# The three looped recurrent units of a one-core hybrid decoder kernel, written out

## What is computed

```python
def step(state, inp):                       # per chunk of 64 tokens and head
    qc, kc, vc, gc = inp
    b = jnp.cumsum(gc, axis=2)
    o_inter = jnp.einsum('bhck,bhkv->bhcv', qc * jnp.exp(b), state)
    ...
    scores = jnp.einsum('bhtk,bhtsk,bhsk->bhts', qc, decay, kc)
    o_intra = jnp.einsum('bhts,bhsv->bhtv', scores, vc)
    k_dec = kc * jnp.exp(b_last - b)
    new_state = jnp.exp(b_last[:, :, 0, :])[..., None] * state + \
        jnp.einsum('bhsk,bhsv->bhkv', k_dec, vc)
    return new_state, o_inter + o_intra
...
o_hg = o_hg * lax.rsqrt(jnp.mean(o_hg * o_hg, axis=-1, keepdims=True) + NORM_EPS) * g
o_hg = o_hg.reshape(B, S, HG_WIDTH) * jax.nn.silu(hg_z)
```

## Time and profile before

| | |
|---|---|
| time, median of 3 runs | 1389.83 us (1387.75 to 1391.33) |
| the profiled execution's own time | 1390.81 us |
| its span in the trace | 1389.0 us |
| TensorE busy | 1311.9 us (94%) |
| VectorE, ScalarE, GpSimd busy | 725.4, 465.1, 433.7 us |
| mean granted TensorE clock | 0.987 of full speed |

### The profile page before, as it was taken

How to read it: one execution, slowest core, us unless ns; L and a number is a source line. 1 busy time by engine, 2 the same in 40 slices (tenths; PEclk the granted TensorE clock), 3 DMA queues, 4 the chain that set the end, 5 groups by cost and what they waited for, 6 DMA issues and landing times.

```text
span 1389.0 us, 24238 instructions
## 1 busy us (share of the span) xinstructions
PE 1311.9 (94%) x8520; PEld 1144.1 (82%) x8520; DVE 725.4 (52%) x1885; ACT 465.1 (33%) x1328; POOL 433.7 (31%) x441
## 2 busy tenths in 40 slices
PE   5999989999999999889999999999999988999997
PEld 5989988998999799888878877887888776778886
DVE  5837674684687367510455454545555455243332
ACT  5621221122212111111454544444544446321111
POOL 5732343233324212120143333333433343112000
PEclk9999999999999999999999999999999999999999
DMA  6520122023002201332354445544544566535431
GB/s 212 149 80 20 47 81 76 20 83 102 23 31 84 84 20 50 97 104 80 73 145 132 114 105 140 132 114 105 155 132 105 145 161 170 168 110 163 143 127 61
DMA packets 121713, 143.92 MB, mean 104 GB/s; under 512 B 20352, under 2 KB 86400, under 8 KB 121600
## 3 DMA queue, kind: packets, MB, share of 16 engines
q1 hardware_dynamic: 119200, 138.46, 35.0%
q10 hardware_dynamic: 2400, 3.93, 1.1%
HBM read 87.56 MB, written 29.62 MB: 84 GB/s over the span
## 4 chain that ended last, share of the span: by engine, by line
PE 41%; DMA 6%; DVE 3%; issue 2%; POOL 2%; SPq 2%; ACT 1%; ACTq 0%; POOLq 0%; DVEq 0%
PE bank L760 4%; PE bank L788 4%; PE bank L762 4%; PE bank L761 4%; PE bank L790 4%; PE bank L789 4%; PE bank L919 3%; PE bank L866 3%; PE bank L859 2%; PE bank L911 2%; PE bank L880 1%; DMA qd<-turned 1%; DMA ks<-turned 1%; PE bank L888 1%; DMA tab<-in_rope 1%
## 5 line engine op out<-in xcount | busy, mean ns | idle before, releaser
L627 PE MATMUL bank<-w_hi,u_hi 128*128 128x256 f32 x768 | 222.7, 290 | 8.6 <-POOL w_lo L1180 4.5
L628 PE MATMUL bank<-w_lo,u_hi 128*128 128x256 f32 x768 | 219.3, 286 | 0.0
L629 PE MATMUL bank<-w_hi,u_lo 128*128 128x256 f32 x768 | 219.2, 285 | 0.0
L1361 DVE TENSOR_TENSOR room<-room 128x256 f32<-128x256 f32 (+6 forms) x386 | 137.1, 403 | 41.3 <-POOL room L1244 37.6
L627 PEld LDWEIGHTS bank<-w_hi,u_hi 128*128 128x128 f32 x768 | 149.4, 195 | 11.2 <-POOL w_lo L1180 4.5
L628 PEld LDWEIGHTS bank<-w_lo,u_hi 128*128 128x128 f32 x768 | 149.5, 195 | 0.2
L629 PEld LDWEIGHTS bank<-w_hi,u_lo 128*128 128x128 f32 x768 | 149.3, 194 | 0.0
L760 PE MATMUL bank<-u_hi,w_hi 128*128 128x512 f32 x256 | 109.6, 428 | 5.5 <-issue 4.0
L627 PE MATMUL bank<-u_hi,w_hi 128*128 128x512 f32 x256 | 101.2, 395 | 7.3 <-issue 3.7
L1361 DVE TENSOR_TENSOR t<-bank,tab 128x512 f32<-128x512 f32 x64 | 42.5, 685 | 120.2 <-DMA tab<-in_rope 58.7
L788 PE MATMUL bank<-u_hi,mT_hi 128*128 128x512 f32 x256 | 102.1, 399 | 2.7 <-DVE mT_lo L1361 2.7
(11 more groups left out here) (169 smaller groups left out, 2950.6 us busy)
## 6 DMA issues: line engine op xcount, KB each, us to landing
qd<-turned SPq DMA_DIRECT2D x64, 256.0 KB, 4.8
stage<-in_w_groups SPq DMA_DIRECT2D x44, 256.0 KB, 3.8
room<-in_x SPq DMA_DIRECT2D x16, 512.0 KB, 4.3
values_gates<-vg_tile SPq DMA_DIRECT2D x64, 128.0 KB, 1.7
room<-values_gates SPq DMA_DIRECT2D x16, 512.0 KB, 4.5
tab<-in_rope SPq DMA_DIRECT2D x16, 512.0 KB, 6.2
wide<-mix_weights SPq DMA_DIRECT2D x32, 256.0 KB, 3.9
xr<-in_x SPq DMA_DIRECT2D x16, 512.0 KB, 5.0
```

Of the source, the lines that this page charges most:

```text
L627: nc.tensor.matmul(dst, lhs_hi(k), rhs_hi(k), start=(k == 0), stop=False)
L628: nc.tensor.matmul(dst, lhs_hi(k), rhs_lo(k), start=False, stop=False)
L629: last = nc.tensor.matmul(dst, lhs_lo(k), rhs_hi(k), start=False, stop=(k == KT_N - 1))
L1361: return nc.vector.tensor_tensor(dst, a_, b_, op)
```

## The change

On each engine the loop over the first three units becomes an ordinary Python loop over all four, so that the same function is written out four times, with `u` a number each time. Nothing else is touched: the steps, their order, buffers and semaphores are those of before, and each unit waits for the same values. SP's helper `after` counts a semaphore up behind a wait on a register's value, and with numbers it does so no more.

```diff
--- before.py
+++ after.py
@@ -434,9 +434,8 @@
                         phase1_store(u + 1, i, last)
 
 
-            with sp.Fori(0, HG_UNITS - 1) as u:
-                hg_unit(u, False)
-            hg_unit(HG_UNITS - 1, True)
+            for u in range(HG_UNITS):
+                hg_unit(u, u == HG_UNITS - 1)
 
             def load_mixed(t):
                 sp.dma_start(mx[t % MX_SLOTS][:, :], mixed_dram[t * P:(t + 1) * P, :]).then_inc(mx_landed[t % MX_SLOTS], 16)
@@ -724,9 +723,8 @@
                     elif kind == "T":
                         phase1_tile(u + 1, b, "hgrn")
 
-            with pe.Fori(0, HG_UNITS - 1) as u:
+            for u in range(HG_UNITS):
                 hg_unit(u)
-            hg_unit(HG_UNITS - 1)
 
 
             def filler_matmuls(kind, n, part):
@@ -1041,9 +1039,8 @@
                     elif kind == "T":
                         phase1_tile(u + 1, b, "hgrn")
 
-            with act.Fori(0, HG_UNITS - 1) as u:
+            for u in range(HG_UNITS):
                 hg_unit(u)
-            hg_unit(HG_UNITS - 1)
 
 
             def queries_keys_hi(n):
@@ -1255,9 +1252,8 @@
                     elif kind == "T":
                         phase1_tile(u + 1, b, "hgrn")
 
-            with pool.Fori(0, HG_UNITS - 1) as u:
+            for u in range(HG_UNITS):
                 hg_unit(u)
-            hg_unit(HG_UNITS - 1)
 
 
             for i in range(4):
@@ -1541,9 +1537,8 @@
                         last.then_inc((out_done0, out_done1)[b % 2], 1)
                 restart()
 
-            with dve.Fori(0, HG_UNITS - 1) as u:
+            for u in range(HG_UNITS):
                 hg_unit(u)
-            hg_unit(HG_UNITS - 1)
 
 
             def classes(ap):
```

## The result

| | before | after |
|---|---|---|
| time, median (range, runs), taken side by side | 1391.38 us (1384.2 to 1398.3, 12) | 1381.24 us (1377.0 to 1383.7, 12) |
| ratio, 95% interval | | 0.9931 (0.9911 to 0.9952) |
| the profiled execution's own time, its span | 1390.81, 1389.0 us | 1379.92, 1377.9 us |
| its mean granted clock | 0.987 | 0.992 |

What follows compares the result with a forecast made beforehand. TensorE, busy 1311.9 of 1389.0 us, was taken as the bound; 1.1 us gained at two seams, nothing elsewhere, took the profiled 1390.8 to 1389.7 us, the median to 1388.7 us, range 1385.8 to 1391.5 us (8 in 10).

Steps and rivals of the forecast that it cites:

- The seams of the changed kernel: Between units: P0 follows O3 without a jump, new waits appear before P1, whose f group starts at 20.02 us.
- the data's chain: From O3 through squares, root, Z3, its store, weight loads and splits to the sigmoids that free P1's f group's bank.
- the mark: Start of O3's first matmul at the end of a unit, from which the prediction counts times at each seam.
- a gain of 1.1 us: At the first two seams together, P1's f group starts earlier: 40.04 us in sum against 41.13 us.
- 21.09, 20.04: Starts in us of P1's f group after O3's first matmul, first and second seam, one profile of the kernel before.
- my rival on the clock: At the seams, longer waits behind P0 and P1 would lower TensorE's clock: slower, 1394.1 us; chance 0.05.
- L688 and the register instructions: Waits before the last block's transposes stay 1.3 to 1.5 us; dropping address arithmetic on VectorE, ScalarE and GpSimd gains nothing.
- Code. ... Nothing is added for that: In the written-out units, the other engines' extra code fetches stay hidden, as in the fourth unit: 0 us.
- The rivals: Four alternatives, 0.24 together: whole gap back, gap not the jump's, slower by clock, slower by code loading on VectorE.
- the whole gap back: At both seams, loads land early enough that the jumps' 3.7 us returns in full: 1386.1 us; chance 0.12.
- a floor of 1385.0: P1's f group at its earliest, 18.14 us after O3's first matmul, at both seams: a gain of 4.9 us.

Runs made afterwards that it cites:

- cut_out: The changed kernel stopped behind the fourth unit, without dense stage, attention and output projection: median 611.46 us, against 612.61 us for the looped kernel cut likewise.
- cut_pe: The kernel before, cut off behind the fourth unit, with only TensorE's units written out: median 612.57 us, against 612.61 us with all loops.
- sp_out: The kernel before with only SP's units written out: the expected gain of 0.5 to 1 us doesn't show; its time isn't given in the text.
- dap_out: The kernel before with only VectorE's, ScalarE's and GpSimd's units written out: slower by 0.24%.
- cut_gap: The changed kernel cut off behind the fourth unit, with TensorE waiting for O3's squares before P0 of units 2 to 4: median 610.97 us, against 611.46 us without that wait.
- loop_match: The kernel before, loops kept, with 48 empty increments under the last unit's matmuls, putting TensorE's later code where the changed kernel has it: 1385.49 us (before 1390.88).
- out_match: The changed kernel with 208 empty increments under the last unit's matmuls, putting TensorE's later code where the kernel before has it: 1385.47 us (before 1390.88).
- loop_tail: The kernel before, loops kept, with 88 empty increments on TensorE under the last unit's matmuls: 1387.33 us, ratio 0.9990 (0.9964 to 1.0016).
- after_again: The changed kernel run unchanged once more for a second profile: 1380.23 us, ratio to the kernel before 0.9937 (0.9912 to 0.9962).
- out_tail: The changed kernel with 166 empty increments on TensorE under the last unit's matmuls: 1389.30 us, ratio to the kernel before 1.0000 (0.9973 to 1.0026).

## Why the prediction was wrong

- **The seams of the changed kernel**: right in mechanism. Without jumps P 0 follows at once, the wait moves to P 1, and the data's chain sets its f group, at 20.0 us behind the mark in the mean of 18 seams, those of the nine full-length profiles with TensorE written out (19.4 to 20.8); the forecast was 20.02. In cut_out and cut_pe it is 20.1 to 21.1.
- **The size of "a gain of 1.1 us"**: too small by one term, "21.09, 20.04": I took the seams of one profile of the kernel before as what its seams are. In the 14 seams of the seven full-length looped profiles the f group starts 21.2 us behind the mark in the mean (20.0 to 22.5), and the second seam of that one profile is the earliest of all. Two seams are worth 2.3 us. I had looked at its clock there (1.00) and did not ask how often it would be otherwise, and my rival on the clock had the sign the wrong way round: it falls at seams with a jump (5 of 16).
- **L688 and the register instructions**: right in the main. The waits at L688 are 1.3, 1.0 and 1.7 us against 1.47, 1.50 and 1.35: 3.9 us in all against 4.3, though two of them lie outside the 1.3 to 1.5 us that I gave. Without their register instructions the other engines gained nothing (sp_out, dap_out).
- **"Code. ... Nothing is added for that"**: this is the step that failed. I asked whether the fetches of the written-out units would stall someone. That part of it was small: one wait has grown, in the second unit. Before and after:

```profile
298.29 0.68 PE L711 MATMUL bank<-room 128*128 128x128 f32 x4 [0.16 <-issue]
```

```profile
298.50 0.71 PE L710 MATMUL bank<-room 128*128 128x128 f32 x4 [0.81 <-ACT room L1030]
```

It is 0.6 to 1.0 us in every profile with ScalarE, VectorE and GpSimd written out, dap_out among them, and 0 to 0.4 us in every other. In each of the former two 8 KB packets of q14 stand in the 2.5 us ahead of it, in none of the latter; that they are its cause is likely and not shown. From P 1's f group to O 3 the second unit takes 105.3 us in the mean of the full-length ones of the former and 104.8 us in that of the others.

What I did not ask is where the fetches behind the units would go once TensorE's code is longer; I took everything behind the fourth unit as unchanged. Moved by itself, with the loops kept, the code's place gave 0.36% (0.11 to 0.62), some 5 us. The Trainium skill ("Runtime: NRT & Kernel Launch", Instruction fetch mechanics) says that the sequencer drives its own DMA queue in blocks of 16 KB and that the cost of crossing a block is mostly hidden. The first agrees with q8 here. The second holds for TensorE itself in the units, where writing out added no gap but those for data, and not for what shares the DMA engine: the store of 2.4 us took 3.5 to 4.4 us.
- **The rivals**: none had it. The one that came nearest in its number (the whole gap back, 1386.1 us, with a floor of 1385.0) was wrong in its mechanism, as cut_gap shows.

The sum afterwards, against 6.5 to 9.6 us (0.9953, 0.9937 and 0.9931 of 1388.5), from the means of the profiles: 2.3 us at the two seams with jumps. 1.2 us elsewhere in the units: P 1's f group starts 19.9 us behind the mark of the third seam where TensorE is written out and 20.6 us where it is looped, though there is no jump in either, and the 544 matmuls up to the first seam take 74.0 us in place of 74.5 us; why, no run shows. About 2.6 us in the turn from the units to the dense stage. That leaves 0.4 to 3.5 us for the attention stage. From the 4,401st to the 8,001st matmul it took 593.1 to 599.8 us in the five profiles with the code at the old place and 592.7 to 600.1 us in the five at the new one, 595.9 and 594.8 us in the mean: of the 6.8 us between the first two profiles, which had sent me there, most was chance. Which wait there turns into a stretch of half clock differs from one profile to the next of the same kernel, and I could not tie it to a packet, so how the code's place acts behind the turn stays open. Nor is the code's share known better than roughly: it is 5.0 us between before and loop_match and 1.9 to 5.0 us between out_match and the three ratios of the changed kernel.

## What to carry to other kernels

Before taking a stage as unchanged because its code is, ask whether the change lengthens or shortens the code ahead of it: fetches of that engine's code then fall elsewhere, and may meet a store or load that others wait for. A kernel that differs by half a per cent can be tested for this by empty instructions under cover of matmuls, which cost nothing there in these runs and show the layout's share; what remains at the same place of the code is the edit's own. One shift isn't enough for that: loop_tail and loop_match, 40 increments apart, gave 0.9990 and 0.9964. And a wait read from one profile is one draw: the looped profiles gave seams from 20.0 to 22.5 us.

## What the runs showed that I had not expected

- TensorE's code comes in packets of 16 KB, mostly one for every 110 to 130 matmuls here, and one of them beside a 256 KB store delays a sixteenth of that store's packets, and with them its end by 1.1 to 2.0 us.
- An empty semaphore increment on TensorE costs 0.15 us at the program's start once there are 80 of them (40 more took the first matmul from 13.13 to 19.27 us), and nothing between matmuls 0.22 us apart.
- Shifting code by less than one block, by 166 such increments and with no other edit, moved the time of this kernel from 1380.2 to 1389.3 us (after_again, out_tail), as much as the whole change did.
